# A fourteenth place for the weights of a light expert turn, and down units that land in another order

## The chip, the cores and the metric

One core of one Trainium2 chip. The metric is the time of one execution on the device, in microseconds (us); smaller is better.

## What is computed

A decoder trunk of two layers on 256 tokens of width 1024, all in float32. The change lies in the last part of layer 2, a mixture of experts (two of eight for each token, feed-forward width 2816):

```python
def swiglu(h, w_gu, w_down):
    g, u = jnp.split(h @ w_gu, 2, axis=-1)
    return (jax.nn.silu(g) * u) @ w_down

def moe_swiglu(h, w_router, b_router, w_gu, w_down):
    ...
    out = jnp.zeros((B * S, D), jnp.float32)
    for e in range(N_EXPERTS):
        out = out + combine[:, e:e + 1] * swiglu(tok, w_gu[e], w_down[e]).astype(jnp.float32)
    return out.reshape(B, S, D).astype(h.dtype)
```

An expert has 1024 x 5632 gate and up weights and 2816 x 1024 down weights, 34.6 MB; all eight are 277 MB of the 405 MB that the kernel moves.

## The kernel before

Layers are worked through one after the other. PE multiplies, ACT and DVE prepare weights and results, and SP issues nearly all weight transfers, on one DMA queue, in the order of its program; it waits on semaphores, and whatever stands behind a waiting issue waits too.

The experts come last, in eight turns. They are sorted by the number of their tokens and placed so that heavy and light ones alternate: turns 0, 2, 4 are heavy, 1, 3, 5 light (`LIGHT = (1, 3, 5, 7)`), turn 6 is a loop over heavy blocks (it runs once here, `LOOP_FROM = 6`), and turn 7, the last, is light.

*Places.* Weights land in `arena`, 11 places (`RING_M`) of one unit each: 128 partitions x 2048 numbers (`UNIT`), 1 MB. A half of the gate and up weights (gate: stage 0, up: stage 1) is eight rows (`KC`) of 128 x 2816 numbers, 1.375 units or 1408 KB, and fills 11 units; the down weights are 11 units too, u0 to u10. So a turn is three laps of 11 units.

*Heavy turns* (`turn_tensor`, up to 128 tokens). ACT rounds each unit into `WH` (`hi_m`, line 1422), DVE takes the rest into `WL` (line 2062), and PE multiplies three times (`mm3`, lines 2182 to 2184). A place is free once DVE has its unit (`lo_ready`). `WH` has three buffers.

*Light turns* (`light_tensor`, up to 64 tokens). PE multiplies the float32 weights as they landed (`both`, line 2696), two halves of the columns side by side, with no help of ACT and DVE. A place is free once PE's product is through (`light_through(stage, k, nth)`: row k of stage 0 or 1, or down unit k for stage 2). Light turns have two places more, which heavy turns use for other things: `extra` (in the memory of `WH`, so free only after the heavy turn's products) and `spare`. That makes thirteen. `light_place` says in which place a column of a half stands. A row that crosses from one tensor to another is cut, in its DMA and in its matmuls (`light_pieces`).

SP's order around the change is that of `load_light_turn` and `load_turn`. In a light turn it issues one unit of gate weights at once, into `spare`, the others when the heavy turn before has left their places (`heavy_down`, lines 752 to 760); then the up rows, behind the gate's products; then down units u0 to u10, each behind the product that frees its place (`LIGHT_DOWN_FREE`). In turns 1 and 3 the next heavy turn's gate rows 0 and 1 are issued between u8 and u9 (`starts_ahead`), the other rows behind down products (`HEAVY_ROW_AFTER`). In turn 5, ahead of the loop, rows 0 and 1 come after all down units too.

```python
        LIGHT_DOWN_AT = (8, 9, 10, None, None, 4, 5, 6, 7, 8, 9)
        LIGHT_DOWN_FREE = ((0, KC - 1), None, (1, 0), (1, 1), (1, 2), (1, 5), (1, 6), (1, 7), None, (2, 0), (2, 1))
        HEAVY_ROW_AFTER = (3, 4, 5, 6, 7, 9, RING_M - 1, RING_M - 1)
```

`LIGHT_DOWN_AT` is the arena place of each down unit (None: `extra`, `spare`), the third table the down unit whose product each heavy row waits for. At the start of a heavy turn ACT's `first_hi` rounds unit 0 (row 0's head, `head_landed`) and `hi_m(1)` unit 1, which ends in row 1.

In the last light turn some small products stand between the down units: lines 2755 and 2762 after u1, u3, u5 and u7 bring earlier parts of the result into the banks, and line 2767 after u6 turns the last one-hot. When u10 is through, ACT copies the result (line 1395), and scatter, norm and store follow.

POOL writes the tokens of each expert into a table in HBM during turn 0 (line 1035, four indirect DMAs) and reads one block back into `ysb` (line 1040).

Of the kernel before, what the change touches and what calls it, by code (L numbers as in the profile page):

```python
# [98 lines left out]
def trunk(nc, x, mem, g_mix, w_in, w_pool, pool_scale, w_dw, b_dw, conv_ln_g, conv_ln_b, w_conv_out,  # L99
# [131 lines left out]
    with ExitStack() as ctx:  # L231
# [59 lines left out]
        WL = sb("WL", [P, HL, UNIT], F32R)  # L291
        xs = sb("xs", [P, NT, D])
# [153 lines left out]
        rows_ahead = mem_in_s  # L446
# [207 lines left out]
        def light_unit(u):  # L654
            if LIGHT_DOWN_AT[u] is None:
                return (extra if u == 3 else spare)[:, :]
            return raw[LIGHT_DOWN_AT[u]]

        def light_pieces(stage, r):

            pieces = []
            for j, (o, w) in enumerate(SEGS):
                cuts = {0, w}
                for start in (r * FF + o, r * FF + FF // 2 + o):
                    for edge in ((UNIT,), (UNIT, 2 * UNIT, 3 * UNIT))[stage]:
# [5 lines left out]

        def starts_ahead(turn):
            return isinstance(turn, int) and turn + 1 < LOOP_FROM
# [23 lines left out]
        def _(sp):  # L697
# [51 lines left out]
            def load_light_turn(e, turn, nth):  # L749
# [18 lines left out]
                load_light_row(e, 1, 0, UNIT, FF, extra_landed)  # L768
                load_light_row(e, 1, 1, 0, 2 * UNIT - FF, extra_landed)
                sp.wait_ge(*light_through(0, 0, nth))  # L770
                load_light_row(e, 1, 1, 2 * UNIT - FF, FF, part_landed[0])
# [103 lines left out]
        def light_extra(s, lights):  # L875

            return 16 * lights * (s == 1)
# [2059 lines left out]
```

## Time and profile before

| | |
|---|---|
| median of 3 runs | 1331.70 us |
| lowest, highest | 1329.79, 1331.94 us |
| profiled execution | 1331.76 us |
| its span, first to last instruction | 1330.0 us |
| mean granted clock of TensorE | 0.997 |
| PE busy | 1309.7 us (98%) |
| DVE, ACT busy | 870.7, 654.8 us |
| bytes moved | 405.39 MB |

Times in the rows below are from the span's start. A matmul's time overlaps the next one's, so PE's pace is read from starts. Float32 products of light turns show as two matmul rows each: a down unit is x8. A DMA's landing is its issue time plus the time given. Arena transfers of 1408 KB are rows of gate or up weights, those of 1024 KB from `in_w_moe_down` down units.

### The profile page before, as it was taken

The numbers are of one execution on the slowest core, as the hardware profiler recorded it, in microseconds if no ns is written. First come the engines' busy times: TensorE is split into PE (matmuls) and PEld (weight loads), VectorE is DVE, ScalarE is ACT, GpSimd is POOL, SyncE is SP. The second block draws the span as 40 slices with busy tenths as digits, with TensorE's granted clock in tenths as the row PEclk, the third lists the DMA queues.
The fourth block names the chain that finished last, engine by engine and source line by source line (L and its number), as shares of the span: only waits on it lengthen the run. The fifth ranks groups of instructions, "written<-read, shape, count | busy, mean of one in ns | idle before, by whom it ended". The sixth has DMA issues, their size and how long they took to land.

```text
span 1330.0 us, 18656 instructions
## 1 busy us (share of the span) xinstructions
PE 1309.7 (98%) x7531; PEld 1029.3 (77%) x7531; DVE 870.7 (65%) x978; ACT 654.8 (49%) x685; POOL 89.3 (7%) x117
## 2 busy tenths in 40 slices
PE   9999999999999999999999999999999999999997
PEld 8999899888888999889888744886448864488632
DVE  6998876654445899887689613896138961389601
ACT  6544664654445454655577403764037640377401
POOL 1003000000000000300075200000000000000000
PEclk9999999999999999999999999999999999999999
DMA  9565965555555555552899999999999999999995
GB/s 315 183 202 184 341 221 162 188 190 190 188 186 164 191 177 169 178 190 80 352 380 416 398 417 421 423 421 421 422 422 424 420 418 422 422 424 421 411 423 213
DMA packets 128531, 405.39 MB, mean 305 GB/s; under 512 B 7454, under 2 KB 76414, under 8 KB 101822
## 3 DMA queue, kind: packets, MB, share of 16 engines
q1 hardware_dynamic: 124142, 392.11, 76.7%
q0 software_dynamic: 2832, 10.75, 2.1%
q10 hardware_dynamic: 1472, 1.34, 0.3%
q8 instruction: 60, 0.98, 0.3%
q14 instruction: 25, 0.20, 0.0%
HBM read 392.64 MB, written 11.53 MB: 304 GB/s over the span
## 4 chain that ended last, share of the span: by engine, by line
PE 90%; DMA 3%; DVE 3%; ACT 3%; issue 1%; POOL 0%; POOLq 0%; DVEq 0%; ACTq 0%; SPq 0%
PE bank L2182 22%; PE bank L2184 22%; PE bank L2183 22%; PE bank L2696 15%; DMA arena<-in_w_moe_gu 3%; ACT WH L1422 1%; DVE WL L2062 1%; PE bank L2663 1%; PE bank L2779 1%; PE bank L2686 1%; PE bank L2729 0%; PE bank L2226 0%; DMA xs<-in_x 0%; PE bank L2603 0%; PE bank L2345 0%
## 5 line engine op out<-in xcount | busy, mean ns | idle before, releaser
L2062 DVE TENSOR_TENSOR WL<-arena,WH 128x2048 fp32r<-128x2048 f32 x126 | 286.5, 2288 | 48.0 <-ACT WH L1422 47.4
L1508 DVE TENSOR_TENSOR WL<-arena,WH 128x2048 fp32r<-128x2048 f32 x108 | 245.1, 2271 | 92.7 <-ACT WH L1080 92.6
L1422 ACT ACTIVATE WH<-arena 128x2048 fp32r<-128x2048 f32 x126 | 241.1, 1921 | 97.6 <-PE bank L2184 85.9
L2182 PE MATMUL bank<-WH,XH 128*128 128x512 f32 (+1 forms) x728 | 273.5, 376 | 4.0 <-DVE WL L2062 3.8
L2183 PE MATMUL bank<-WL,XH 128*128 128x512 f32 (+1 forms) x728 | 269.5, 370 | 0.0
L2184 PE MATMUL bank<-WH,XL 128*128 128x512 f32 (+1 forms) x728 | 268.9, 369 | 0.0
L1080 ACT ACTIVATE WH<-arena 128x2048 fp32r<-128x2048 f32 x109 | 206.3, 1894 | 75.5 <-PE bank L2184 62.0
L2182 PE MATMUL bank<-XH,WH 128*128 128x256 f32 x592 | 168.1, 284 | 0.4 <-DVE XL L1538 0.4
L2184 PE MATMUL bank<-XH,WL 128*128 128x256 f32 x592 | 167.5, 283 | 0.0
L2183 PE MATMUL bank<-XL,WH 128*128 128x256 f32 x592 | 167.5, 283 | 0.0
L2182 PEld LDWEIGHTS bank<-WH,XH 128*128 128x128 f32 x728 | 137.6, 189 | 33.7 <-issue 6.9
L2184 PEld LDWEIGHTS bank<-WH,XL 128*128 128x128 f32 x728 | 137.3, 189 | 23.8
L2183 PEld LDWEIGHTS bank<-WL,XH 128*128 128x128 f32 x728 | 137.8, 189 | 21.9
L2696 PE MATMUL bank<-arena,XF 128*64 128x512 f32 (+2 forms) x680 | 139.4, 548 | 0.0
L2182 PEld LDWEIGHTS bank<-XH,WH 128*128 128x128 f32 x592 | 113.6, 192 | 0.7 <-issue 0.6
L2696 PEld LDWEIGHTS bank<-arena,XF 128*64 128x64 f32 x680 | 50.7, 137 | 81.7 <-issue 81.7
L2183 PEld LDWEIGHTS bank<-XL,WH 128*128 128x128 f32 x592 | 113.6, 192 | 0.2
L2184 PEld LDWEIGHTS bank<-XH,WL 128*128 128x128 f32 x592 | 113.6, 192 | 0.0
L1572 DVE SCALAR_TENSOR_TENSOR arena<-arena,vec 128x256 f32<-128x256 f32 x240 | 97.9, 476 | 0.0
L2048 DVE TENSOR_TENSOR sgm<-sgm,bank 128x512 f32<-128x512 f32 x8 | 5.5, 687 | 104.6 <-PE bank L2696 104.6
L942 POOL TENSOR_TENSOR rs<-vv,mhalf 128x2 f32<-128x2 f32 x8 | 5.6, 706 | 965.5 <-DVE vv L2151 585.0
L2696 PE MATMUL bank<-arena,hTf 128*64 128x512 f32 x288 | 65.3, 597 | 4.0 <-DMA arena<-in_w_moe_down 4.0
(393 smaller groups left out, 1786.8 us busy)
## 6 DMA issues: line engine op xcount, KB each, us to landing
arena<-in_w_moe_gu SPq DMA_DIRECT2D x109, 1408.0 KB, 12.7
arena<-in_w_moe_down SPq DMA_DIRECT2D x76, 1024.0 KB, 14.5
arena<-in_w_in SPq DMA_DIRECT2D x27, 1024.0 KB, 5.0
arena<-in_w_ffn_gu SPq DMA_DIRECT2D x44, 512.0 KB, 4.8
arena<-in_w_xkv SPq DMA_DIRECT2D x16, 1024.0 KB, 5.1
arena<-in_w_ffn_down SPq DMA_DIRECT2D x11, 1024.0 KB, 4.9
xrows<-hTl POOLq DMA_DIRECT2D x8, 1024.0 KB, 9.3
arena<-in_w_mix_out SPq DMA_DIRECT2D x8, 1024.0 KB, 9.3
```

Source lines behind the costliest of these rows:

```text
L1080: a.activation(WH[:, n % HL, 0:width(n)], s[:, 0:width(n)], ACT.Copy).then_inc(hi_ready, 1)
L1422: a.activation(WH[:, (NA + i) % HL, :], raw[i % RING_M], ACT.Copy).then_inc(hi_ready, 1)
L1508: v.tensor_tensor(WL[:, n % HL, 0:w], s[:, 0:w], WH[:, n % HL, 0:w].bitcast(F32), ALU.subtract).then_inc(lo_ready, 1)
L1572: v.scalar_tensor_tensor(acc[:, c, :], cu[:, c, k:k + S], tap(L, k, c), acc[:, c, :], ALU.mult, ALU.add).then_inc(conv_step, 1)
L2062: v.tensor_tensor(WL[:, (NA + i) % HL, :], raw[i % RING_M], WH[:, (NA + i) % HL, :].bitcast(F32), ALU.subtract).then_inc(lo_ready, 1)
L2182: te.matmul(out, ah, bh, start=start, stop=False, skip_group_check=shared)
L2183: te.matmul(out, ah, bl, start=False, stop=False, skip_group_check=shared)
L2184: return te.matmul(out, al, bh, start=False, stop=stop, skip_group_check=shared)
L2663: ins = te.matmul(ps[:, c * slots:c * slots + slots], xn[:, t, kk * P:kk * P + P], PM[:, t, 0:slots], start=(c, t) == (0, 0), stop=(c, t) ...
L2686: ins = te.matmul(bank[b][:, :], hotT[rows_at, t, :], half[rows_at, ms], start=half is yh, stop=half is yl)
L2696: ins = te.matmul(outs[r * HALF:r * HALF + HALF], lefts, rights[r], start=start, stop=stop, skip_group_check=shared)
L2779: ins = te.transpose(ps[:, c * P:c * P + P], heavy_sg(j)[:, f + c % 2:f + 2 * P:2], ident[:, :])
```

## The change

A new tensor `more` (1 MB) is the fourteenth place. To make room for it, the ring for the DMAs that POOL issues is set to 4096 (`dynamic_dma_scratch_size`). `light_place` puts gate columns into `spare`, `more`, then the arena, and up columns into arena places 9 and 10, `extra`, `spare`, `more`, then the arena from place 0. At its start a light turn issues 2 MB without waiting for the arena. The down units get places 6, 7, 8, 9, `extra`, 3, 4, 5, 10, `spare` and `more`, and are issued in the order 0, 1, 2, 3, 8, 4, 9, 10, 5, 6, 7; PE multiplies them in the order 0 to 10 as before. The next heavy turn's rows come behind all down units in every turn: rows 0 and 1 wait for up products (rows 4 and 5), row 2 for u6's product, row 3 for u7's, rows 4 and 5 for none, row 6 for u8's. `first_hi` waits for u4's product (that unit is in `extra` now). The rest are counts of semaphores that follow from it.

```diff
@@
+        more = sb("more", [P, UNIT])
@@
-        LIGHT_DOWN_SEM = (8, 9, 10, 0, 1, 2, 3, 4, 5, 6, 7)
-        LIGHT_DOWN_AT = (8, 9, 10, None, None, 4, 5, 6, 7, 8, 9)
-        LIGHT_DOWN_FREE = ((0, KC - 1), None, (1, 0), (1, 1), (1, 2), (1, 5), (1, 6), (1, 7), None, (2, 0), (2, 1))
-        HEAVY_ROW_AFTER = (3, 4, 5, 6, 7, 9, RING_M - 1, RING_M - 1)
+        LIGHT_DOWN_SEM = (8, 9, 10, 5, 7, 2, 3, 4, 6, 0, 1)
+        LIGHT_DOWN_AT = (6, 7, 8, 9, extra, 3, 4, 5, 10, spare, more)
+        LIGHT_DOWN_ORDER = (0, 1, 2, 3, 8, 4, 9, 10, 5, 6, 7)
+        LIGHT_DOWN_FREE = {0: (0, KC - 2), 1: (0, KC - 1), 3: (1, 0), 8: (1, 1), 4: (1, 2), 9: (1, 3), 10: (1, 4),
+                           5: (1, KC - 2), 6: (1, KC - 1)}
+        HEAVY_ROW_AFTER = ((1, 4), (1, 5), (2, 6), (2, 7), None, None, (2, 8), None)
@@ light_place
-            if c < UNIT:
-                return (spare, c) if stage == 0 else (arena, 10 * UNIT + c)
             if stage == 0:
-                return arena, c - UNIT
+                return (spare, c) if c < UNIT else (more, c - UNIT) if c < 2 * UNIT else (arena, c - 2 * UNIT)
             if c < 2 * UNIT:
-                return extra, c - UNIT
-            return (spare, c - 2 * UNIT) if c < 3 * UNIT else (arena, c - 3 * UNIT)
+                return arena, 9 * UNIT + c
+            if c < 5 * UNIT:
+                return (extra, spare, more)[c // UNIT - 2], c % UNIT
+            return arena, c - 5 * UNIT
@@ load_light_turn
                 load_light_row(e, 0, 0, 0, UNIT, spare_landed)
+                load_light_row(e, 0, 0, UNIT, FF, spare_landed)
+                load_light_row(e, 0, 1, 0, 2 * UNIT - FF, more_landed)
                 heavy_down(0)
-                load_light_row(e, 0, 0, UNIT, FF, part_landed[0])
-                for r in range(1, KC):
-                    heavy_down((r * FF + FF - UNIT - 1) // UNIT)
-                    load_light_row(e, 0, r, 0, FF, part_landed[r])
+                load_light_row(e, 0, 1, 2 * UNIT - FF, FF, part_landed[0])
+                for r in range(2, KC):
+                    heavy_down((r * FF + FF - 2 * UNIT - 1) // UNIT)
+                    load_light_row(e, 0, r, 0, FF, part_landed[r - 1])
                 heavy_down(RING_M - 1)
-                load_light_row(e, 1, 0, 0, UNIT, slot_landed)
+                load_light_row(e, 1, 0, 0, FF, slot_landed)
+                load_light_row(e, 1, 1, 0, 2 * UNIT - FF, extra_landed)
...
-                for r in range(3, KC):
-                    sp.wait_ge(*light_through(0, r - 1, nth))
-                    load_light_row(e, 1, r, 0, FF, part_landed[r - 1])
-                for u in range(RING_M):
-                    if LIGHT_DOWN_FREE[u]:
+                for r in range(4, KC):
+                    sp.wait_ge(*light_through(0, r - 2, nth))
+                    load_light_row(e, 1, r, 0, FF, part_landed[r - 3])
+                for u in LIGHT_DOWN_ORDER:
+                    if u in LIGHT_DOWN_FREE:
                         stage, r = LIGHT_DOWN_FREE[u]
                         sp.wait_ge(*light_through(stage, r, nth))
...
-                    if u == 9 and starts_ahead(turn):
-                        after = expert_at(turn + 2)
-                        load_first_row(after, rows_ahead)
-                        load_row(after, 0, 1, rows_ahead)
                     load_light_down(e, u)
@@ first_hi
-                    act.wait_ge(*light_through(2, 3, LIGHT.index((turn if isinstance(turn, int) else LOOP_FROM) - 1)))
+                    act.wait_ge(*light_through(2, 4, LIGHT.index((turn if isinstance(turn, int) else LOOP_FROM) - 1)))
@@ kernel
-    nc = bacc.Bacc("TRN2", target_bir_lowering=False, num_devices=1)
+    nc = bacc.Bacc("TRN2", target_bir_lowering=False, num_devices=1, dynamic_dma_scratch_size=4096)
```

How the instructions stand. First SP at the start of light turn 1 (ISA rows compute an address; waits are named by semaphore). Before:

```order
L735 DMA spare<-in_w_moe_gu 128x2048
L735 ISA [waits lo_ready]
L735 DMA arena<-in_w_moe_gu 128x768
L735 ISA [waits lo_ready]
L735 DMA arena<-in_w_moe_gu 128x2816
```

and now:

```order
L734 DMA spare<-in_w_moe_gu 128x2048
L734 ISA
L734 DMA more<-in_w_moe_gu 128x768
L734 ISA
L734 DMA more<-in_w_moe_gu 128x1280
L734 ISA [waits lo_ready]
L734 DMA arena<-in_w_moe_gu 128x1536
L734 ISA [waits lo_ready]
L734 DMA arena<-in_w_moe_gu 128x2816
```

Two more pieces stand ahead of the first wait for the heavy turn's places (`lo_ready`). Then SP at the end of light turn 1, from u8 on before:

```order
L747 DMA arena<-in_w_moe_down 128x2048
L845 TENSOR_LOAD order [waits light_part_used]
L845 ISA x2
L793 ISA
L793 DMA arena<-in_w_moe_gu 128x2048
L794 ISA
L794 DMA arena<-in_w_moe_gu 128x768
L726 ISA
L726 DMA arena<-in_w_moe_gu 128x2816
L747 ISA
L747 DMA arena<-in_w_moe_down 128x2048
L742 ISA [waits light_part_used]
```

and from the second half of u10 on now:

```order
L741 DMA more<-in_w_moe_down 128x1024
L746 ISA [waits light_part_used]
L746 DMA arena<-in_w_moe_down 128x2048
L746 ISA [waits light_gu_done]
L746 DMA arena<-in_w_moe_down 128x2048
L746 ISA
L746 DMA arena<-in_w_moe_down 128x2048
L847 TENSOR_LOAD order
L847 ISA x2
L793 ISA [waits light_part_used]
L793 DMA arena<-in_w_moe_gu 128x2048
L794 ISA
```

The heavy turn's first rows (lines 793, 794 and 726) stood ahead of u9 and u10; now u5, u6 and u7 are the last down units, and the rows follow them. Last PE's down products in light turn 1 (four matmuls a unit; line 2671 turns a one-hot), before:

```order
L2696 MATMUL bank<-arena,hTf 64x512 x8
L2671 MATMUL bank<-ident,PM 128x128 x2
L2696 MATMUL bank<-arena,hTf 64x512 x4
L2696 MATMUL bank<-extra,hTf 64x512 x4
L2696 MATMUL bank<-spare,hTf 64x512 x4
L2696 MATMUL bank<-arena,hTf 64x512 x24
```

and now:

```order
L2702 MATMUL bank<-arena,hTf 64x512 x8
L2677 MATMUL bank<-ident,PM 128x128 x2
L2702 MATMUL bank<-arena,hTf 64x512 x8
L2702 MATMUL bank<-extra,hTf 64x512 x4
L2702 MATMUL bank<-arena,hTf 64x512 x16
L2702 MATMUL bank<-spare,hTf 64x512 x4
L2702 MATMUL bank<-more,hTf 64x512 x4
```

The units are multiplied in the same order, from other places; the x16 are u5 to u8, and u9 and u10 are in `spare` and `more`. On POOL and DVE no instruction moves.

## Rows read from the trace of the kernel before

**Rows 1.** The page's part 2, whole span in 40 slices

```profile
GB/s 315 183 202 184 341 221 162 188 190 190 188 186 164 191 177 169 178 190 80 352 380 416 398 417 421 423 421 421 422 422 424 420 418 422 422 424 421 411 423 213
```

**Rows 2.** Chain of waits, 1140 to 1160 us (start, us, what)

```profile
1142.09 10.80 DMA arena<-in_w_moe_gu
...
1152.99 1.93 ACT WH L1422
```

**Rows 3.** Waits of PE, 1160 to 1322 us (total, times, longest)

```profile
PE bank L2913 <- ACT ysb L1395: 0.8, 1, 0.8
PE bank L2182 <- DVE WL L2062: 0.2, 1, 0.2
```

**Rows 4.** Timeline, PE and ACT, last down products (start, us, what)

```profile
1305.04 1.89 PE L2696 MATMUL bank<-arena,hTf 128*64 128x512 f32 x8
...
1310.15 1.94 PE L2696 MATMUL bank<-arena,hTf 128*64 128x512 f32 x8
...
1319.62 0.60 ACT L1395 ACTIVATE ysb<-bank 128x512 f32<-128x512 f32 x1 [8.97 <-PE bank L2696]
```

**Rows 5.** DMA issues, median us to landing, issued 1293.14 and 1298.33

```profile
arena<-in_w_moe_down SPq DMA_DIRECT2D x1, 1024.0 KB, 14.1
...
arena<-in_w_moe_down SPq DMA_DIRECT2D x1, 512.0 KB, 13.9
```

**Rows 6.** Windows, us, PE busy, clock, DMA share, GB/s; turns 1, 3, 5, 7

```profile
740.00:770.00 30.00, 30.00 (x146) 1.00 0.99 385
905.00:935.00 30.00, 30.00 (x147) 1.00 1.01 421
1070.00:1100.00 30.00, 30.00 (x148) 1.00 1.01 416
1236.00:1266.00 30.00, 29.85 (x149) 1.00 1.00 409
```

**Rows 7.** SP's issues in light turn 1, and us to landing of the last

```profile
753.74 0.88 SPq L735 DMA_DIRECT2D extra<-in_w_moe_gu  x2
759.79 2.69 SPq L735 DMA_DIRECT2D spare<-in_w_moe_gu  x2
...
spare<-in_w_moe_gu SPq DMA_DIRECT2D x1, 768.0 KB, 6.5
```

**Rows 8.** DMA issue to an empty queue, issued 663.74

```profile
arena<-in_w_moe_gu SPq DMA_DIRECT2D x1, 1408.0 KB, 5.9
```

**Rows 9.** DMA issues at 805.98 and 813.48, us to landing

```profile
arena<-in_w_moe_gu SPq DMA_DIRECT2D x1, 1408.0 KB, 11.2
...
arena<-in_w_moe_gu SPq DMA_DIRECT2D x1, 1408.0 KB, 12.1
```

**Rows 10.** DMA issues at 917.95 and 918.46, us to landing

```profile
extra<-in_w_moe_gu SPq DMA_DIRECT2D x1, 384.0 KB, 10.3
...
extra<-in_w_moe_gu SPq DMA_DIRECT2D x1, 640.0 KB, 12.3
```

**Rows 11.** Timeline of PE, down products of light turn 1

```profile
811.40 4.03 PE L2696 MATMUL bank<-arena,hTf 128*64 128x512 f32 x18
...
819.68 3.65 PE L2696 MATMUL bank<-arena,hTf 128*64 128x512 f32 x16 [1.24 <-DMA arena<-in_w_moe_down]
```

**Rows 12.** Timeline of PE, start of heavy turn 6

```profile
1152.14 0.50 PE L2182 MATMUL bank<-WH,XH 128*128 128x512 f32 x1
...
1157.36 0.70 PE L2182 MATMUL bank<-WH,XH 128*128 128x512 f32 x1 [2.20 <-DVE WL L2062]
```

**Rows 13.** Windows with the granted clock, start of heavy turn 6

```profile
1155.00:1160.00 5.00, 2.80 (x9) 0.75 1.00 424
```

**Rows 14.** POOL's timeline; DMA issues; PE's reading of ysb

```profile
716.18 0.62 POOL L1040 DMA_DIRECT2D ysb<-xrows  x1 [12.71 <-DMA xrows<-xn,dest]
...
xrows<-xn,dest POOLq DMA_INDIRECT x4, 11.7
...
742.55 0.38 PE L2792 MATMUL bank<-ident,ysb 128*128 128x128 f32 x2
```

More of the change, by code:

```diff
@@ L654, in light_unit @@
         def light_unit(u):
-            if LIGHT_DOWN_AT[u] is None:
-                return (extra if u == 3 else spare)[:, :]
-            return raw[LIGHT_DOWN_AT[u]]
+            at = LIGHT_DOWN_AT[u]
+            return raw[at] if isinstance(at, int) else at[:, :]
         def light_pieces(stage, r):
@@ L664, in light_pieces @@
                 for start in (r * FF + o, r * FF + FF // 2 + o):
-                    for edge in ((UNIT,), (UNIT, 2 * UNIT, 3 * UNIT))[stage]:
+                    for edge in ((UNIT, 2 * UNIT), (2 * UNIT, 3 * UNIT, 4 * UNIT, 5 * UNIT))[stage]:
                         if start < edge < start + w:
@@ L670, in light_pieces @@
             return pieces
-        def starts_ahead(turn):
-            return isinstance(turn, int) and turn + 1 < LOOP_FROM
         def heavy_sg(j):
@@ L793, in load_first_row @@
                 sp.dma_start(arena[:, 0:UNIT], src[:, 0:UNIT]).then_inc(head_landed, 16)
-                sp.dma_start(arena[:, UNIT:FF], src[:, UNIT:FF]).then_inc(rest_landed, 16)
+                sp.dma_start(arena[:, UNIT:FF], src[:, UNIT:FF]).then_inc(rows_ahead, 16)
             def row_end(r):
@@ L802, in load_turn @@
                         continue
-                    if HEAVY_ROW_AFTER[r] is not None:
-                        sp.wait_ge(*light_through(2, HEAVY_ROW_AFTER[r], LIGHT.index(
-                            (turn if isinstance(turn, int) else LOOP_FROM) - 1)))
+                    if HEAVY_ROW_AFTER[r]:
+                        stage, k = HEAVY_ROW_AFTER[r]
+                        sp.wait_ge(*light_through(stage, k, LIGHT.index((turn if isinstance(turn, int) else LOOP_FROM) - 1)))
                     if not isinstance(turn, int):
                         sp.wait_ge(lo_ready, heavy(turn, NM, max(NA - RING_M + row_end(r) + 1, LOOP_FROM // 2 * NM)))
-                    if r < 2 and isinstance(turn, int):
-                        sp.sem_inc(part_landed[r], 16)
-                    elif r:
-                        load_row(e, 0, r)
-                    else:
-                        load_first_row(e, part_landed[0])
+                    if r:
+                        load_row(e, 0, r, rows_ahead if r == 1 else None)
+                    else:
+                        load_first_row(e)
+                if gate_rows:
+                    sp.wait_ge(*light_through(2, RING_M - 1, LIGHT.index((turn if isinstance(turn, int) else LOOP_FROM) - 1)))
+                    for k in range(2):
+                        sp.sem_inc(part_landed[k], 16)
                 for r in range(KC):
@@ L875, in light_extra @@
         def light_extra(s, lights):
-            return 16 * lights * (s == 1)
+            return 16 * lights * (s in (0, 7))
         def lights_before(turn):
@@ L891, in light_row_in @@
         def light_row_in(stage, r, turn, nth):
-            if stage and r == 0:
-                return extra_landed, 32 * nth + 32
-            s = r - stage
-            return part_landed[s], upto(turn, 48, 16 * stage + 16 + light_extra(s, nth + stage))
+            if stage == 0:
+                if r == 0:
+                    return spare_landed, 32 * nth + 32
+                return part_landed[r - 1], upto(turn, 48, 16 + light_extra(r - 1, nth))
+            if r < 2:
+                return (extra_landed, 32 * nth + 32) if r else (slot_landed, 16 * nth + 16)
+            s = 7 if r == 2 else r - 3
+            return part_landed[s], upto(turn, 48, (48 if r < 4 else 32) + light_extra(s, nth))
         def light_down_in(u, turn, nth):
@@ L1414, in hi_m @@
                 def hi_m(i):
-                    if i == 1 and isinstance(turn, int) and turn:
-                        act.wait_ge(rows_ahead, 16 + 16 * turn)
+                    if i == 1 and not (isinstance(turn, int) and turn == 0):
+                        act.wait_ge(rows_ahead, heavy(turn, 32, 16))
                     else:
@@ L2709, in light_tensor @@
                             pe.wait_ge(g_lo, upto(turn, 2, 3 + r // 2))
-                        if r == 0:
-                            pe.wait_ge(slot_landed if stage else spare_landed, 16 * nth + 16)
+                        if (stage, r) == (0, 1):
+                            pe.wait_ge(more_landed, 16 * nth + 32)
                         pe.wait_ge(*light_row_in(stage, r, turn, nth))
```

20 lines of the change are left out of this document (11 added, 9 removed).

## The prediction

> **What bounds the kernel now.** I read the page's slices first. PE is busy in all of them; the queue moves about 420 GB/s, but only from the 22nd slice on, where the experts' weights stream [rows 1]. A busy PE is no proof there, so I read next, in the chain of waits, what the start of a heavy turn hangs on. Turn 6 starts on a row of expert weights: issued 1142.09, landed 1152.89, then ACT's 1.93 us and DVE's split, and PE goes on at 1157.36 [rows 2, 12]. Up to there the weight stream sets the pace. After it no transfer holds PE again: from 1160 to 1322 it waits 1.0 us in all, for ACT and DVE [rows 3]. It ends its last product at 1319.6, where ACT takes the result [rows 4]. The last weights landed at 1298.3 + 13.9 = 1312.2, 7.4 us before [rows 5].
>
> So two lengths set the end: when the stream brings turn 6's second row, and what PE needs from there. The stream is full nearly always. Four equal stretches around the change from heavy to light show where not: 385, 421, 416 and 409 GB/s in turns 1, 3, 5 and 7 [rows 6]. Against 421 they lack (421 - 385)/421 x 30 = **2.6 us** in turn 1, 0.4 in turn 5, 0.9 in turn 7. The issue times say why in turn 1: SP stops after 754.6 until 759.79, and the 768 KB issued then land in 6.5 us [rows 7]. A row given to an empty queue took 5.9 [rows 8], so there the queue had run almost dry; in the filled stream a row takes 10.8 to 12.1 [rows 2, 9].
>
> **The change, part by part.**
>
> *A fourteenth place.* Row 0 and 5 KB per partition of row 1 (2 MB, before 1 MB) go out at a light turn's start without a wait, and each later piece of both halves waits for one place less. SP is 1 MB ahead, 2.5 us of stream. That is more than the empty stretch of turn 7 and about that of turn 1, so I count nearly all: 2.6 in turn 1, 0.4 in turn 5, both ahead of turn 6's start; 0.9 in turn 7, behind it.
>
> *More pieces.* A light turn has 22 DMAs for its gate and up rows where 20 were. Pieces of 384 and 640 KB, issued together at 917.95 and 918.46, landed at 928.25 and 930.76 [rows 10]: the second took 2.5 us at most, where 640 KB at 421 GB/s are 1.6. The rest is at least in part the tail of the first. I take 0.1 us a turn; bounds 0 and 0.3.
>
> *Down units in another order.* Before, u0 to u10 land in the order in which PE multiplies them, and rows 0 and 1 of the next heavy turn stand ahead of u9 and u10 (turns 2 and 4). Now the landing order is 0, 1, 2, 3, 8, 4, 9, 10, 5, 6, 7, PE's is as it was, and heavy row 0 follows u7. So u5, u6 and u7 land in the ninth to eleventh place where they were sixth to eighth, 7.5 us later. In turns 2 and 4 the same bytes lie ahead of row 2 as before, so the stream is not longer. PE takes 3.6 us for two units (x16) and waited for u9 and u10 anyway, 1.24 us at 819.68 [rows 11]; now it waits at u5 to u7 and has u8 to u10 at once. Light turn 1 ends about 822 by that, 819.68 + 3.6 = 823.3 before: nothing lost.
>
> *The wait of row 2 on u6's product.* Behind it on SP stand rows 3 to 7. In turn 1 PE has u6 multiplied at about 814.9 (u5 starts 811.40, 1.8 each) [rows 11]. Row 1 landed at 805.98 + 11.2 = 817.2 before, with u9 and u10 (5 us) behind it; now these are ahead of it, less the 2.6 gained: lands 819.6, its last bytes some 2 us earlier. The issue of row 2 at 815.1 leaves 2.5 us of stream. That is about the state in which the 6.5 us piece was issued, so I charge **0.3 us**; bounds 0 and 1. In turns 3 and 5 SP waits for PE, which waits for u6's landing; u7 and rows 0 and 1 are then still to come, 9 us of stream less 4 for landing, product and issue: full.
>
> *Turn 6's start.* Its row 0 came behind all down units already, so its place in the stream does not move. It lands earlier by 2.6 + 0.4 - 0.3 - 0.3 (three turns' pieces) = **2.4 us**. PE: u7 lands where u10 did, ahead of rows 0 and 1 (2.75 MB, 6.9 us at 421 GB/s), at 1146.0 less 2.4; u7 to u10 take 7.2, unit 0 of turn 6 3.0 (from 1152.14 to 2.2 before 1157.36 [rows 12]); PE is through with it at 1156.2 less 2.4, about one us before the second row is split. So the start moves by the full 2.4. Before, PE idled 2.2 us there and its granted clock fell, to 0.75 in the mean of 1155 to 1160, between its levels of 2.4 and 1.2 GHz [rows 13]; the matmul at 1157.36 took 0.70 us where the one at 1152.14 took 0.50 [rows 12]. At half speed until 1160.6 that is 1.7 us lost. With one us of idling the clock may not fall; counted at nothing, for the reason next.
>
> *The end.* Here the new order costs. Last turn, landings before: ninth unit 1293.14 + 14.1 = 1307.2, eleventh 1312.2, the tenth halfway at 1309.7 [rows 5]. Now these are u5, u6, u7, earlier by 2.4 and by 0.8 of turn 7 (0.9 less its pieces): 1304.0, 1306.5, 1309.0. PE would want u5 at 1305.04 - 2.4 = 1302.6 [rows 4]: it waits 1.4. Then u5 1.8 and L2762 1.1: u6 at 1306.9 (landed 1306.5); 1.8 and, for the transposes, 0.4: u7 at 1309.2 (landed 1309.0), against 1310.15 before. From u7's start to the end nothing changes (9.5 us to the result), so the gain of 2.4 is worth 0.9 us at the end, **0.8** with the release of a wait. A PE that comes sooner only waits longer for u5: that is why the clock is counted at nothing. The cuts that the new edges make in light matmuls (two a turn) stand before that wait and are covered by it; without the cover, eight instructions at the pace of rows 4 (1.89 for 8) are 1.9 us.
>
> *A smaller ring for POOL's DMAs* (4096, to make room). After its last scatter POOL idles 12.71 us for the landing; PE reads what the reload at 716.18 brings at 742.55 [rows 14]. That is 26 us, less a landing of 6 to 12 [rows 8, 9]: 14 to 20 of room. Cost 0; bound in rival C. POOL's order is the same. The Trainium skill ("SBUF — State Buffer", its size table) tells of a 16 KiB carveout for this ring; no row here shows its size.
>
> **Sum.** The profiled execution took 1331.76 us by its time (span 1330.0), the median of three is 1331.70. 1331.8 - 0.8 = **1331.0 us**. About 0.2% (2.7 us) can be told from no change in this kernel: no difference that can be measured.
>
> **Rivals.**
>
> A, *faster: the late units don't bind.* If the stream gains all it lacks, 2.6 + 0.4 + 0.9 = 3.9, with pieces and the thin place free, and u5 to u7 are in time, PE's own gain counts: 3.0 at the start and up to 1.7 of clock, so 1331.7 - 4.7 = 1327.0; with half the clock 1328. For it: the dip of turn 1 is plain. Against: the landings of rows 5, which follow from bytes and rate, leave PE 1.4 us of waiting even so. Decided by PE's idle time ahead of u5. Chance 0.18.
>
> B, *slower: the last turn waits and the clock falls.* If the dips are not a dry queue but other traffic, the stream gains nothing. Then u7 lands at 1312.2, so its product starts 2.1 later than now, and if the clock falls on the wait at u5 as it did on 2.2 us of idling at 1155, another 1.7 is lost: 1331.7 + 3.8 = 1335.5. For it: the late units are sure. Against: turns 1 and 7 dip where SP pauses [rows 6, 7]. It leaves the 0.2% only with both, no gain and the fallen clock. Chance 0.09.
>
> C, *slower: the small ring* holds one scatter at a time. Then three of the four wait out the 11.7 us of another's landing [rows 14]: up to 35 later, 15 to 21 beyond the room, 1346 to 1352. Against: nothing in the trace shows POOL waiting between its scatters. Chance 0.02.
>
> D, *slower: each piece costs its fixed time.* The row given to the empty queue took 5.9 us where its 1.44 MB at 421 GB/s are 3.4 [rows 8]: 2.5 fixed. If that were paid for each of the eight extra DMAs, two in each of four light turns, it would be 1331 + 20 = 1351. Against: in the full queue the pieces of rows 10 landed 2.5 apart in all. Chance 0.01. The Trainium skill ("DMA: Bandwidth & Descriptors", Anatomy of one DMA) states such a fixed cost, about 2.0 us per DMA, most of it the receipt of the last byte; by that, paid in full, the change would cost 16 us, and the trace disagrees for a full queue.
>
> **How the numbers follow.** My own case has 0.70, with what ends near it (gain and late units cancelling, 1331 to 1333). Its terms' bounds: before turn 6 the stream gains from 3.0 - 1.0 - 0.9 = 1.1 to 3.0, in turn 7 from 0.6 to 0.9. The end follows u7's landing, 2.1 later than now with no gain, so it lies 0.4 above to 1.8 below 1331.7; with the runs' own scatter of one us 1329 to 1333. Reaching into A and B: 1328.4 to 1333.4. Faster by over 0.2% 0.18, within 0.70, slower 0.12.
>
> **What would show it.** In the profile of after: stretches like rows 6 at 419 or more in turns 1, 5 and 7, else the place gains nothing; the piece after 759 landing in over 8 us; the second row of turn 6 landing near 1150.5; PE idle 1 to 2 us ahead of the sixth down unit of the last turn, and the three units after it without idling; the result taken 9.5 us after u7's start. I am wrong if PE doesn't wait there (A), if the dip of turn 1 stays (B), or if PE's transposes of ysb in turn 0 start after 745 (C), or if the stretches of rows 6 fall below before in turn 3 (D).

## The result and the profile after

The changed kernel is slower, by a little more than can be told from no change, and lies outside the predicted range.

| | before | changed |
|---|---|---|
| median | 1330.55 us (10 runs) | 1333.93 us (10 runs) |
| lowest, highest | 1329.79, 1331.94 | 1332.20, 1335.87 |
| ratio, 95% interval | | 1.0021 [1.0012, 1.0030] |
| profiled execution (its span) | 1331.76 us (1330.0) | 1335.87 us (1334.1) |

The medians alone lie 3.4 us apart; the interval covers 1.6 to 4.0 us. The ten runs of the changed kernel fall into two groups. Three had 1332.20 to 1332.37 and one 1333.0, at a granted clock of 0.998 to 0.999 over the span; the other six had 1333.88 to 1335.87, at 0.996 to 0.997. The profiled one is the slowest of them.

First the stretches of [rows 6] in the changed kernel, and three with the clock (us, PE busy, granted clock, DMA share, GB/s):

```profile
740.00:770.00 30.00, 30.00 (x151) 1.00 1.01 419
905.00:935.00 30.00, 30.00 (x150) 1.00 1.01 419
1070.00:1100.00 30.00, 30.00 (x154) 1.00 1.00 408
1155.00:1160.00 5.00, 3.87 (x19) 1.00 1.02 430
...
1236.00:1266.00 30.00, 29.85 (x152) 1.00 1.01 420
1305.00:1310.00 5.00, 2.50 (x6) 0.74 0.82 340
1310.00:1315.00 5.00, 5.00 (x22) 0.92 0.09 35
```

The fourteenth place did what it should to the rate: 385 GB/s became 419 in turn 1 and 409 became 420 in turn 7. In this execution turn 5 did not gain (416 before, 408 now); in the profiles of a0, e1, e4 and e7 below it ran at 419 to 420. The clock of 0.75 at turn 6's start [rows 13] is gone; a new one, 0.74, stands at 1305, at the end.

Did the faster queue bring turn 6's second row earlier? Before it was issued at 1142.09 and landed at 1152.89 [rows 2]. Now it is issued ten us earlier, at 1132.33 (DMA issues of that moment, median us to landing):

```profile
arena<-in_w_moe_gu SPq DMA_DIRECT2D x1, 1408.0 KB, 20.5
```

1132.33 + 20.5 is 1152.86: nothing gained, where 2.4 us were forecast. PE starts on the unit behind it at the same moment as in [rows 12], though it has idled half as long (timeline of PE):

```profile
1157.34 0.49 PE L2188 MATMUL bank<-WH,XH 128*128 128x512 f32 x1 [1.13 <-DVE WL L2068]
```

The matmul takes 0.49 us, not 0.70: this is the clock that now stays up. With it the last light turn's matmuls start at 1253.46, where they started at 1254.50 before. So the changed kernel enters the last turn 1.0 us ahead, and leaves it 4.1 behind. PE's waits from 1160 to 1326:

```profile
PE bank L2702 <- DMA arena<-in_w_moe_down: 3.3, 1, 3.3
PE bank L2919 <- ACT ysb L1401: 0.8, 1, 0.8
PE bank L2188 <- DVE WL L2068: 0.4, 2, 0.2
```

and the chain of waits there (start, us, what):

```profile
1289.23 18.22 DMA arena<-in_w_moe_down
...
1307.50 3.54 PE bank L2702 x8
1311.04 1.06 PE bank L2768 x4
1312.10 1.87 PE bank L2702 x8
...
1314.34 1.87 PE bank L2702 x8
...
1323.73 0.61 ACT ysb L1401
```

[Rows 3] has no wait for a transfer; here is one, for a down unit: u5, issued at 1289.23, landed 18.22 us later. Its eight product rows take 3.54 us where eight take 1.87 two lines below. That is the fallen clock: 1.7 us. ACT takes the result at 1323.73; in [rows 4] it was 1319.62.

### The profile page after: what moved, and what is told of

The parts are those of the page before. It is cut to its first block, busy times and chain, and to the rows that moved or that the text cites. A ratio compares the mean times of both kernels' runs of the same rounds, so it can differ in the third digit from the quotient of the medians.

```text
span 1334.1 us, 18743 instructions
## 1 busy us (share of the span) xinstructions
PE 1311.2 (98%) x7563; PEld 1031.3 (77%) x7563; DVE 870.9 (65%) x978; ACT 655.0 (49%) x685; POOL 87.0 (7%) x117
## 4 chain that ended last, share of the span: by engine, by line
PE 87%; DMA 6%; ACT 3%; DVE 2%; issue 1%; SPq 0%; POOL 0%; POOLq 0%; DVEq 0%; ACTq 0%
PE bank L2188 22%; PE bank L2190 22%; PE bank L2189 22%; PE bank L2702 13%; DMA arena<-in_w_moe_gu 4%; DMA arena<-in_w_moe_down 1%; ACT WH L1428 1%; DVE WL L2068 1%; PE bank L2692 1%; PE bank L2785 1%; PE bank L2232 0%; DMA xs<-in_x 0%; PE bank L2609 0%; PE bank L2351 0%; PE bank L2877 0%
## 5 line engine op out<-in xcount | busy, mean ns | idle before, releaser
L2702 PE MATMUL bank<-arena,XF 128*64 128x512 f32 (+3 forms) x616 | 130.8, 543 | 0.0
L2188 PE MATMUL bank<-WH,hThm 128*128 128x512 f32 x160 | 65.2, 407 | 0.0
```

Source lines behind the costliest of these rows:

```text
L2188: te.matmul(out, ah, bh, start=start, stop=False, skip_group_check=shared)
L2702: ins = te.matmul(outs[r * HALF:r * HALF + HALF], lefts, rights[r], start=start, stop=stop, skip_group_check=shared)
```

## The experiments

Each was timed beside the kernel before, e5 in four runs, the others in ten or eleven. "Before" had a median of 1331.02 us beside a0, e1, e3 and e4 (33 runs), 1331.32 beside e2, e5 and e6 (21), 1331.24 beside e7 and e8 (20).

| kernel | median us (lowest, highest) | ratio to before, 95% |
|---|---|---|
| a0 changed kernel again | 1334.21 (1332.77, 1336.65) | 1.0024 [1.0015, 1.0033] |
| e1 last turn's units in order | **1329.53** (1329.18, 1330.14) | 0.9987 [0.9978, 0.9996] |
| e2 before, small ring | 1331.22 (1329.63, 1331.93) | 0.9998 [0.9989, 1.0007] |
| e3 changed, places held back | 1334.94 (1332.28, 1335.81) | 1.0027 [1.0018, 1.0036] |
| e4 changed, PE kept busy at u5 | 1332.75 (1332.31, 1333.46) | 1.0013 [1.0004, 1.0022] |
| e5 before, one engine loaded | 1337.65 (1336.74, 1339.27) | 1.0043 [1.0028, 1.0059] |
| e6 before, PE kept busy at turn 6 | 1331.02 (1329.48, 1331.97) | 0.9997 [0.9988, 1.0006] |
| e7 e1 and e3 together | 1329.56 (1329.13, 1331.00) | 0.9989 [0.9980, 0.9998] |
| e8 before, last turn reordered | 1335.21 (1334.07, 1337.36) | 1.0030 [1.0021, 1.0039] |

### a0: the changed kernel once more

No edit.

> The changed kernel again, beside the experiments of the same chip. Theory T (the late units u5 to u7 of the last turn hold PE, and the clock falls on that wait in some executions): 1332.2 to 1335.9 again, two groups 1.7 us apart; PE idles 2 to 4 us ahead of the sixth down unit of the last turn; the second row of turn 6 lands at 1152.5 to 1153.5. Rival R (the 3 us come from somewhere before turn 6): PE's idle time ahead of that unit would be below 1 us in executions of 1334 and more.

Measured 1334.21 us, 3.2 above before. PE's waits from 1160 to 1326 again begin with the same line:

```profile
PE bank L2702 <- DMA arena<-in_w_moe_down: 3.2, 1, 3.2
```

Here u5 landed at 1305.78, 1.7 us earlier than in the first profile, but PE was ready for it earlier by as much (1302.65 against 1304.19), so the wait is as long. The result was taken at 1321.92.

### e1 and e8: the order of the last turn, taken out and put in alone

e1 is the changed kernel with

```diff
-                for u in LIGHT_DOWN_ORDER:
+                for u in LIGHT_DOWN_ORDER if isinstance(turn, int) else range(RING_M):
```

> The changed kernel with the down units of the last turn alone issued as u0 to u10, so that they land in PE's order. T: PE isn't held in the last down products, the 3.3 us of waiting and the 1.7 of fallen clock go, and the gain at the start of turn 6 (0.97) stays: the result is taken at 1318.5 to 1319, time 1329.0 to 1330 us, 4 below the slower group of the changed kernel and at or just below the kernel before. R: 1333 to 1334 as the changed kernel.

Its windows and PE's waits from 1120 to 1326:

```profile
1155.00:1160.00 5.00, 3.59 (x18) 1.00 1.01 428
...
1305.00:1310.00 5.00, 5.00 (x24) 1.00 0.80 324
```

```profile
PE bank L2188 <- DVE WL L2068: 1.7, 3, 1.2
PE bank L2702 <- DMA arena<-in_w_moe_down: 1.1, 2, 0.6
PE bank L2919 <- ACT ysb L1401: 0.8, 1, 0.8
```

PE waits for no transfer in the last turn (the 1.1 us are in turn 5, in two pieces), the clock stays up at both places, and the result is taken at 1318.00. At 1329.53 us it is faster than both kernels.

e8 is the other way round: the kernel before, with the new order in the last turn only (u8 then needs the wait that u7 had).

```diff
-                for u in range(RING_M):
-                    if LIGHT_DOWN_FREE[u]:
-                        stage, r = LIGHT_DOWN_FREE[u]
+                for u in range(RING_M) if isinstance(turn, int) else (0, 1, 2, 3, 8, 4, 9, 10, 5, 6, 7):
+                    free = (1, KC - 1) if u == 8 and not isinstance(turn, int) else LIGHT_DOWN_FREE[u]
+                    if free:
+                        stage, r = free
```

> The kernel before with one part of the change alone: the down units of the last light turn are asked for in the order 0, 1, 2, 3, 8, 4, 9, 10, 5, 6, 7. Up to turn 6 nothing differs, so the last light turn's matmuls start near 1254.5 as before. Unit 5 lands at about 1307.2, unit 7 at 1312.2, and PE wants unit 5 at 1305.0. If the cost of the new order is this wait and the fallen clock, PE waits 1.8 to 2.8 us ahead of unit 5, the result is taken at 1321.7 (clock up) to 1323.4 (clock fallen), and the time is 1333.3 to 1335.2, 2 to 4 above before. If the changed kernel's loss came from somewhere else in the change (pieces, thin place, the turns before), this kernel stays within 1 us of before.

Timeline of PE in e8, with the row's idle time and what ended it, and a window:

```profile
1305.63 3.61 PE L2697 MATMUL bank<-arena,hTf 128*64 128x512 f32 x8 [2.29 <-DMA arena<-in_w_moe_down]
...
1310.23 1.94 PE L2697 MATMUL bank<-arena,hTf 128*64 128x512 f32 x8
```

```profile
1305.00:1310.00 5.00, 4.37 (x12) 0.66 1.00 415
```

1335.21 us, 4.0 above before. The edit of one turn's order in an otherwise old kernel gives the whole loss and more, with the same two signs: a wait ahead of u5 (2.29 us) and eight products of 3.61 us. So the account is: the new order of the last turn costs 4.0 (e8) or, taken out of the changed kernel, 4.7 (a0 less e1); the rest of the change gains 1.5 (e1 against before). Together that is 2.5 to 3.2. Measured were 3.2 (a0) and 3.4; each has an interval of about 1.2 us to either side.

The traces show the two parts apart. For each profile, from the chains of waits: when the last turn's first product starts, when ACT takes the result, and the time between.

| kernel | begins | result taken | between |
|---|---|---|---|
| before | 1254.50 | 1319.62 | 65.1 |
| e2 | 1254.38 | 1319.49 | 65.1 |
| e6 | 1253.98 | 1319.10 | 65.1 |
| e1, e7 | 1252.87, 1252.31 | 1318.00, 1317.44 | 65.1 |
| e8 | 1252.60 | 1321.93 | 69.3 |
| changed, a0 | 1253.46, 1251.93 | 1323.73, 1321.92 | 70.3, 70.0 |
| e4 | 1253.23 | 1321.29 | 68.1 |
| e3 | 1255.93 | 1321.58 | 65.7 |

With the units in order the last turn takes 65.1 us in every profile; the new order adds 4.2 to 5.2 where nothing else is done about it. In e3's profile PE came so late that it waited only 0.3 us for u5. The starts scatter: e8, with the code of before up to the last turn, began 1.9 us ahead of before's profile, and its clock stayed up at turn 6. So what "the rest of the change" gains can't be read from one profile of each; it rests on the medians.

### e4: how much of it is the clock

The changed kernel, with PE given three products that nobody reads ahead of u5:

```diff
+                    if u == 4 and last:
+                        for _ in range(3):
+                            te.matmul(bank[4][:, :], ident[:, :], xs[:, 0, 0:512], start=True, stop=True)
```

> The changed kernel with three products more (128x512, into a bank nobody reads, results unchanged) between u4 and u5 of the last turn, about 3.2 us on PE, where it waits for u5. If the fall of the granted clock comes from that idle time: the clock stays at its upper level in 1305 to 1315, u5 takes 1.9 instead of 3.5 us, and the time is 1332.0 to 1332.8 without the slower group (median 1.0 to 1.7 below the changed kernel's). If the clock falls for another reason: u5 takes 3.5 still and the time is the changed kernel's or above.

Timeline of PE in e4:

```profile
1303.89 2.84 PE L2765 MATMUL bank<-xs,ident 128*128 128x512 f32 x6
1306.66 1.94 PE L2702 MATMUL bank<-arena,hTf 128*64 128x512 f32 x8
```

(The trace shows six instructions for the three.) The idle stretch is filled, the clock is 1.00 from 1305 to 1315, and u5's products take 1.94 us. The median falls from 1334.21 to 1332.75, so the fallen clock is worth about 1.5 us, or a little more: in this profile u5 had landed at 1305.69, 1.0 us before the added products let it start. The late landing stays, and the kernel is still slower than before.

### e3 and e7: is the fourteenth place worth anything

e3 lets the light rows wait as if the place were not there, in all light turns:

```diff
+                heavy_down(0)
                 load_light_row(e, 0, 1, 0, 2 * UNIT - FF, more_landed)
-                heavy_down(0)
+                heavy_down(1)
                 load_light_row(e, 0, 1, 2 * UNIT - FF, FF, part_landed[0])
                 for r in range(2, KC):
-                    heavy_down((r * FF + FF - 2 * UNIT - 1) // UNIT)
+                    heavy_down((r * FF + FF - UNIT - 1) // UNIT)
...
-                    sp.wait_ge(*light_through(0, r - 2, nth))
+                    sp.wait_ge(*light_through(0, r - 1, nth))
```

> The changed kernel, where each piece of a light turn's gate and up rows waits as it did before the change: the fourteenth place is there, but nothing is issued earlier for it. S (landings go by the slowest of the transfer engines, which stays busy through the dips of the mean rate; the earlier issue brings only the others forward): the dip of turn 1 is back (385 to 395 GB/s in 740 to 770), the second row of turn 6 still lands at 1152.5 to 1153.5, and the time is within 0.7 us of the changed kernel's. Q (the earlier issue gained its 2.4 us and something else in the change ate them): that row lands near 1155.3 and the time is 2.4 us above the changed kernel's.

```profile
740.00:770.00 30.00, 30.00 (x151) 1.00 1.01 410
...
1160.00:1165.00 5.00, 3.46 (x13) 0.75 1.01 426
1236.00:1266.00 30.00, 29.85 (x151) 1.00 1.01 413
```

The edit brought the dip only partly back (410 GB/s, not 385 to 395), so it is a weaker test than it was meant to be. Turn 6's second row landed at 1152.08, not later than with the place in use. The median is 0.7 us above a0's, within what can be told, and not the 2.4 of theory Q. In this profile PE waited 1.3 and then 1.9 us at turn 6 and its clock fell behind the second wait, not at u5.

e7 has the edits of e1 and e3 both.

> The changed kernel with both earlier edits in one: the light rows wait as if the fourteenth place were not there, and the last light turn brings its down units in the order in which PE multiplies them. If the earlier issue of the light rows is worth nothing at the end, and the lead of the kernel with the last turn in order (1.5 us below before) comes from the down order in turns 1, 3 and 5 (short waits for units in place of one long wait at turn 6), this kernel keeps that lead: 1329.0 to 1330.3 us, clock 1.00 from 1155 to 1165. If the lead comes from the fourteenth place, it is lost: 1330.8 to 1331.8, the same as before. In both cases PE waits under 1.0 us for transfers in the last turn.

```profile
740.00:770.00 30.00, 30.00 (x151) 1.00 1.01 412
...
1155.00:1160.00 5.00, 3.57 (x19) 1.00 1.02 428
```

1329.56 us against e1's 1329.53. With part of the place's earlier issue taken back (412 GB/s in turn 1, where the changed kernel has 419 and kernels with the code of before 385 to 403), the lead is kept in full. So nothing speaks for the earlier issue, the point of the place, as its source. By elimination it comes with the order of the down units in turns 1, 3 and 5, with the heavy rows behind them; no run has that order alone. What e7 shows of how: from 1120 on PE waits three times for the split, 1.3 us at most, and twice for down units, 0.6 at most, where before it waited 2.2 us at once [rows 12] and the clock fell. In turn 3 of the changed kernel's own timeline of PE, three waits stand where before there was one of 2.7 us, but a new one follows at the start of turn 4, for DVE (with a window behind it):

```profile
975.56 1.94 PE L2702 MATMUL bank<-arena,hTf 128*64 128x512 f32 x8 [0.42 <-DMA arena<-in_w_moe_down]
...
978.06 1.94 PE L2702 MATMUL bank<-arena,hTf 128*64 128x512 f32 x8 [0.56 <-DMA arena<-in_w_moe_down]
...
980.54 3.65 PE L2702 MATMUL bank<-arena,hTf 128*64 128x512 f32 x16 [0.55 <-DMA arena<-in_w_moe_down]
...
992.35 0.49 PE L2692 MATMUL bank<-yh,XL 64*128 64x512 f32 x2 [1.77 <-DVE yl L1987]
```

```profile
990.00:995.00 5.00, 3.23 (x14) 0.83 1.02 430
```

The clock fell behind that one. It cost nothing by turn 6, where PE waits for the stream anyway; it brought PE there later, and so made its wait shorter.

### e6: the clock at turn 6 alone

The kernel before, with four products that nobody reads at PE's wait in turn 6:

```diff
+                    if i == 1 and not isinstance(turn, int):
+                        for _ in range(4):
+                            te.matmul(bank[4][:, 0:256], ident[:, :], tri_ones[:, :], start=True, stop=True)
```

> The kernel before with four products more (256 columns, into a bank nobody reads, results unchanged, 2.1 us) between unit 0 and unit 1 of heavy turn 6, where PE idled 2.2 us and its clock fell. If the idle time makes the clock fall and the fall costs what the changed kernel won there (0.97 us at the start of the last light turn): the clock stays up in 1155 to 1165, the last light turn starts near 1253.5, the time is 1329.5 to 1330.3 (0.7 to 1.2 below before), which is where the changed kernel with the last turn in order stands. If that one's lead over before came from the fourteenth place: no change here, 1330.5 to 1331.5.

```profile
1155.00:1160.00 5.00, 5.00 (x25) 1.00 1.00 421
1160.00:1165.00 5.00, 5.00 (x27) 1.00 1.01 422
```

```profile
1156.78 1.89 PE L2809 MATMUL bank<-tri_ones,ident 128*128 128x256 f32 x8
1158.32 0.58 PE L2182 MATMUL bank<-WH,XH 128*128 128x512 f32 x1
```

The clock was held, but the median moved by -0.3 us, within what can be told; I had expected 0.7 to 1.2. The profile says why at least in part. In this execution PE came to the wait 1.8 us later than in [rows 12]: it had waited 2.8 us in turn 3, and the clock from 980 to 990 was 0.83. Then the idle time left was shorter than the four products, and unit 1 started at 1158.32, 0.96 us after [rows 12]; how much of that is a later landing isn't known, as the second row's has no record. Even so the last light turn began at 1253.98, 0.5 us before that of before. The held clock thus gave 1.5 us, and the later start took 1.0.

That e1's lead is the clock at turn 6 is likely, but not shown. For it: e1's highest of eleven runs is 1330.14, while the 33 of before beside it reach from 1329.61, near e1's median, to 1333.05. Against its being all: e1's profile enters the last turn 1.6 us ahead of before's, and 0.6 of that is an earlier landing (unit 1 starts at 1156.77, not 1157.36).

### e2: the smaller ring

The kernel before with the ring of 4096 for POOL's DMAs.

```diff
-    nc = bacc.Bacc("TRN2", target_bir_lowering=False, num_devices=1)
+    nc = bacc.Bacc("TRN2", target_bir_lowering=False, num_devices=1, dynamic_dma_scratch_size=4096)
```

> The kernel before with the smaller ring for POOL's DMAs (4096) and nothing else of the change. If the ring costs nothing: 1330.5 to 1331.5, as before; POOL's idle time for its last scatter stays at 12 to 13 us. If it holds the scatters or slows the stream in turn 0 (the changed kernel's down units of turn 0 landed 1.6 us later than before): POOL idles longer, and the time is 1 to 2 us above before.

1331.22 us against 1331.32: it costs nothing. The run gave something else. Its window of turn 1 reads

```profile
740.00:770.00 30.00, 30.00 (x149) 1.00 1.00 403
```

where the same code had 385 in [rows 6]. Kernels that are the same as before in turn 1 had 385, 403, 389 (e6) and 398 (e8). The dip that I priced at 2.6 us was one execution's; the mean of the four, 394, would have been (421 - 394)/421 x 30 = 1.9. In turn 7 the same four had 409, 403, 422 and 421: the lack of 0.9 us there was that of some executions only.

### e5: load on few of the 16 transfer engines

Why do landings not follow the rate? My theory was that a row has landed only when the last of the 16 transfer engines has its share through, so that landings go by the slowest engine, and the rate by the mean of all. e5 is the kernel before with a small transfer (61 rows of 1 KB, from HBM to HBM) ahead of each of turns 1 to 5.

```diff
+            def one_engine():
+                sp.dma_start(waste, w_moe_down[0][0, 0:61, 0:256]).then_inc(waste_in, 16)
```

> The kernel before with one small DMA more ahead of each of turns 1 to 5, 61 rows of 1 KB from HBM to HBM (62 KB, 0.15 us of the stream's mean each, 0.7 us in all), cut so that few or one of the 16 transfer engines carries it. S (landings go by the slowest engine's own work, not by the mean rate): each costs that engine's whole time for 62 KB, 2 to 5 us less at first the lead that it had, so the second row of turn 6 lands 8 to 25 us after 1152.9 and the kernel is slower by as much. M (landings go by bytes over the mean rate, as the prediction reckoned): 0.7 us later, 1331 to 1332.

Measured: 1337.65 us, 6.3 above before (3.7 to 7.9 by the interval, from four runs), for 0.3 MB in 277. The chain of waits at turn 6, and PE's waits from 1120:

```profile
1146.22 12.93 DMA arena<-in_w_moe_gu
...
1159.26 1.92 ACT WH L1429
```

```profile
PE bank L2189 <- DVE WL L2069: 3.3, 2, 3.1
```

The second row landed at 1159.15, against 1152.89 before: 6.3 us. (This profiled execution took 1339.27, 7.5 more than that of before; after the wait of 3.1 us its clock fell as well.) In the trace the 61 packets of each such transfer follow one another without a gap for 2.6 us, about what a single engine would show (their own times add up to 2.8 us; the trace does not name the engine). Five of them hold that engine for some 14 us; shared out over 16 engines this would be 0.9. The 6.3 lie between: short of the 8 to 25 that I had forecast by the theory, and far more than the mean's 0.7.

The packets, added up from the kept traces, allow a finer reading. For a transfer I take the moment at which the queue had moved as many bytes as had been asked for up to its end, whichever they were ("bytes"), and set the landing beside it. Turn 6's second row, and the last down unit of the kernel:

```
                  turn 6, row 1            eleventh down unit of the last turn
                  bytes    landed   lag    bytes    landed   lag
before            1150.74  1152.89  2.1    1310.11  1312.19  2.1
e2                1150.25  1152.73  2.5    1310.02  1312.74  2.7
e6                1151.84  no record      1310.47  1312.50  2.0
e8                1150.39  1151.97  1.6    1309.93  1311.73  1.8
changed           1149.69  1152.86  3.2    1308.80  1312.38  3.6
a0                1148.77  1151.34  2.6    1308.32  1310.68  2.4
e1                1148.97  1152.29  3.3    1308.22  1311.76  3.5
e3                1149.88  1152.08  2.2    1310.31  1311.87  1.6
e4                1149.16  1152.62  3.5    1308.43  1310.62  2.2
e7                1149.15  1151.71  2.6    1308.61  1311.14  2.5
e5                1154.55  1159.15  4.6
```

The first four rows are code of before, the next six have the change or most of it. In their means (where there are both numbers) the changed ones are ahead by bytes, 1.2 us at turn 6 (1150.5 and 1149.3) and 1.3 at the end (1310.1 and 1308.8; e3 gains nothing there). Of that, landings show 0.4 at turn 6 (1152.5 and 1152.1) and 0.9 at the end: the lag grew from 2.1 to 2.9 and from 2.2 to 2.6. These are few executions with a scatter of about one us, and e3 has a small lag at both places. In e5 the lag is 4.6. The Trainium skill ("DMA: Bandwidth & Descriptors", "Why a DMA increments its semaphore by 16 and not by 1") says that a transfer is split over up to 16 engines and that only the full count of their increments means that its data has landed; e5 agrees with that. That a small load whose packets go one after another delays landings more than bytes is shown.

The larger lag of the changed kernels can be seen in the traces too, since they have the time of each of a transfer's sixteen increments. The first and the last, of the tenth down unit to land in the last turn:

```
            first    last               first    last
before     1306.95  1309.70   changed  1304.25  1309.92
e2         1307.06  1310.28   a0       1302.47  1308.22
e6         1306.89  1310.00   e1       1303.76  1309.26
e8         1307.64  1308.08   e3       1306.95  1309.40
                              e4       1303.34  1308.15
                              e7       1303.06  1308.65
```

In the mean the first share came 3.2 us earlier (1307.1 and 1304.0), as much as I had forecast for whole units, and the last 0.6 (1309.5 and 1308.9). In the changed kernels (e3 apart) the shares that land first got further ahead, and the one that ends a landing hardly gained: what raised the mean rate went past it. Which engine carries it, and why it is behind, the traces do not show.

## Why the prediction was wrong

**"So there the queue had run almost dry" and the gain of 2.4 us before turn 6: wrong.** The rates of turns 1 and 7 rose as forecast (419 and 420). But the step from rate to landing failed, in two ways. The lack of [rows 6] was read from one execution, 385 and 409 GB/s in turns 1 and 7, where others of the same code had 389 to 403 and 403 to 422. And a mean rate was taken for the landing of a transfer, which waits for its last share. By bytes the stream came 1.2 us earlier to turn 6 and 1.3 to the end, not 2.4 and 3.2. And of these the landings showed only 0.4 and 0.9, as the first shares of the transfers gained and the last ones hardly did. The landing of u5 shows it best: forecast for 1304.0; the bytes up to it were through at 1303.47 in the changed kernel's profile and 1302.62 in a0, even before my time. It landed at 1307.45 and 1305.78.

**"It waits 1.4": right place, wrong size.** PE idled ahead of the sixth unit and for no transfer after it in the last turn. PE wanted u5 at 1302.6 in a0 as forecast, and at 1304.2 in the first profile; the wait was 3.2 and 3.3 us. A landing late by 1.8 (a0) goes straight into the end.

**"That is why the clock is counted at nothing": wrong, and the step that moved the sign.** I had seen the clock fall on 2.2 us of idling [rows 13], took its return at turn 6 to be covered by the wait at u5, and did not ask what that wait would do to the clock itself in my own case, only in rival B. At 1.4 us it might have stayed up: it did at turn 6 with idling of 1.1 (changed), 1.2 (a0, e1, e4), 1.3 (e7) and 1.4 us (e8), and fell there with 1.9 (e3, 1.3 us of idling just before), 2.2, 2.8 (e2) and 3.1 (e5). At u5 it fell on 3.3, 3.2 and 2.3 us (e8). Cost: 1.5 us (e4), where rival B said 1.7.

Together: the result was forecast for 1318.8 (1319.6 less 0.8). In a0 it came at 1321.92, 3.1 later; the late landing (1.8) and the clock (1.5) make 3.3. The median missed by 2.9 us.

**Rival B, at 0.09, is what happened** in the profiled execution: no gain in the landings, u5 to u7 as late as the old ninth to eleventh unit, and the fallen clock; its 1335.5 is near that execution's 1335.87. The median, 1333.9, is lower. In a0's profile u5 and u7 landed 1.4 to 1.5 us earlier than the old ninth and eleventh unit, and the kernel still lost 2.3 us to the profiled one of before. I called it unlikely because it needed both; but the second follows from the first. A late landing makes the wait long, and a long wait is what drops the clock. The two should have had one chance between them, not a product.

**Turn 6's start:** the forecast gain of one us at the end was made of an earlier landing. A gain came, but by another way: a wait of 1.1 us in place of 2.2, on which the clock stayed up. The second row landed no earlier; PE came later, to unit 0 at 1153.19 and not 1152.14, since it had waited for DVE and run at the fallen clock at the start of turn 4 (in e1, e4 and e7 it also waited 0.8 to 1.1 us for down units in turn 5). The last turn began 1.0 us earlier by the clock alone.

**Right:** row 2 of turn 2 was issued at 815.35 (forecast 815.1) and nothing behind it suffered. The small ring costs nothing (e2); rival C is out. The extra pieces do not cost their fixed time: e1 has them all and is the fastest; rival D is out. (The Trainium skill's figure that is named there, "DMA: Bandwidth & Descriptors", Anatomy of one DMA, is fitted on transfers that GpSimd issues; these are SP's.) From u7's start to the result it took 9.5 us (1314.27 to 1323.73), as forecast. One sign I gave was missed: the piece behind 759 landed in 6.9 us, not over 8, and yet the rate had no dip, so that a short time to landing is no proof that the rate dips.

## What to carry to other kernels

Bring weights in the order in which they are multiplied at the end of a kernel, where nothing behind can absorb a late landing; an order that cost nothing measurable in the middle (turns 1, 3 and 5) cost 4.0 us in the last turn. Do not turn a gap in the mean rate of transfers into time at the end: look at the landing that the engine waits for, in more than one execution, since a landing waits for the last share of its transfer: here the first shares came 3.2 us earlier and the last 0.6. And price a new wait on PE together with its clock: at the end of this kernel a wait of 2.3 us or more (a0, changed, e8) cost another 1.5 to 1.7.

## What the runs showed of the hardware

- A transfer of 61 KB whose packets run one after another (2.6 us) delayed later landings by over one us (e5: five of them, 6.3 us).
- In the dip of turn 1 the transfer engines were not idle: the DMA share there was 0.99 at 385 GB/s [rows 6]. In the trace of before, 28 of the 452 packets of 11 KB that start from 745 to 770 took over one and a half times their usual 0.42 us (the longest 1.57); in the changed kernel it was 1 of 561. Why packets stretch when few are asked for ahead, the runs do not show.
- At turn 6 the granted clock did not fall after PE had idled 1.1 to 1.4 us (six kernels). Between 1.7 and 2.8 us it was a matter of the execution. At the start of turn 4 the same wait for DVE, 1.7 to 1.8 us, left it up in e1, e3, e4 and e7, and brought it to 0.83 in the changed kernel and 0.66 in a0 (mean of 990 to 995), between its levels of 2.4 and 1.2 GHz. In turn 3, 2.2 us (e2) and 2.7 us (before) left it up, while 2.7 us (e8) and 2.8 us (e6) brought it to 0.68 and 0.66 (985 to 990). After 3.1 to 3.8 us it fell in every one of the profiles above. Three products that nobody reads kept it up (e4), and so did four (e6). So the same kernel may or may not pay in one execution, which may be what parts the runs of the changed kernel into two groups; that was not tried.
- A fall in the middle need not show at the end: in e8 the clock fell in turn 3, and unit 1 of turn 6 still started at 1156.45, 0.9 us sooner than in before, whose clock had stayed up there.
